# A combine in fp32r with a low part, single and half chunks of expert weights, and a norm vector spread by TensorE

## The reference, cut to what matters

```python
h = h + W_o( sum_i sigmoid(G_i xn) * P_i(mixer_i(xn)) )      # xn = RMSNorm(h)
h = h + hier_moe(rms_norm(h, norm2_g), ...)
return rms_norm(h, final_norm_g)

def hier_moe(x, wg, bg, we, be, w1, w3, w2):
    ...   # one of 4 groups, then the 2 best of its 8 experts: combine (256 x 32)
    for e in range(N_EXPERTS):
        h = jax.nn.silu(xt @ w1[e]) * (xt @ w3[e])
        out = out + combine[:, e:e + 1] * (h @ w2[e])
```

## Time and profile before

| | us |
|---|---|
| median of 3 runs | 423.47 (423.26 to 424.98) |
| the profiled execution | 424.43 |
| its span | 422.6 |
| TensorE busy | 392.2 (93%) |
| VectorE / ScalarE / GpSimd busy | 200.6 / 141.8 / 20.1 |
| bytes moved | 140.3 MB, 332 GB/s over the span |
| mean granted clock of TensorE | 0.985 |

### The profile page before, as it was taken

One profiled execution on the slowest core, in us unless ns is written; L12 is line 12 of the kernel. 1 busy time (PEld: TensorE's weight loads), 2 busy tenths in 40 slices (PEclk: granted clock), 3 DMA queues, 4 the chain that ended last, 5 costly groups with the idle time before them and its releaser, 6 DMA issues.

```text
span 422.6 us, 7127 instructions
## 1 busy us (share of the span) xinstructions
PE 392.2 (93%) x2826; PEld 263.9 (62%) x2826; DVE 200.6 (47%) x392; ACT 141.8 (34%) x257; POOL 20.1 (5%) x39
## 2 busy tenths in 40 slices
PE   6999999999999999999989999999999779679792
PEld 5998988677777777878765545453546335135251
DVE  3847574999888595673362323231222203112113
ACT  6734352638555535341430303030303012011014
POOL 3010000200000000000510000000000000000002
PEclk9999999999999999999999999999999989899898
DMA  8999999534352485569987999999999999999962
GB/s 295 421 406 352 399 382 395 198 136 158 106 186 99 152 347 200 205 243 365 420 359 268 433 425 426 410 424 426 426 428 428 426 426 430 426 428 426 430 267 99
DMA packets 16440, 140.29 MB, mean 332 GB/s; under 512 B 2081, under 2 KB 2465, under 8 KB 5025
## 3 DMA queue, kind: packets, MB, share of 16 engines
q1 hardware_dynamic: 15264, 138.07, 81.1%
q10 hardware_dynamic: 1152, 1.88, 1.2%
HBM read 138.90 MB, written 1.05 MB: 331 GB/s over the span
## 4 chain that ended last, share of the span: by engine, by line
PE 73%; DMA 18%; DVE 6%; issue 1%; POOL 0%; ACT 0%; POOLq 0%; DVEq 0%; SPq 0%
DMA ring<-in_experts 17%; PE bank L1758 10%; PE bank L1719 5%; PE bank L1785 5%; PE bank L1795 5%; PE bank L1525 5%; PE bank L1526 4%; PE bank L1527 4%; PE bank L1383 4%; PE bank L1384 4%; PE bank L1385 4%; PE bank L1646 2%; PE bank L1368 2%; PE bank L1647 2%; PE bank L1648 2%; PE bank L1487 1%
## 5 line engine op out<-in xcount | busy, mean ns | idle before, releaser
L1758 PE MATMUL bank<-ring,kv 128*32 128x512 f32 x512 | 65.9, 630 | 12.9 <-DMA ring<-in_experts 12.8
L458 DVE TENSOR_TENSOR part<-ring,part 128x2048 fp32r<-128x2048 f32 (+1 forms) x26 | 57.4, 2213 | 18.7 <-ACT part L451 18.6
L451 ACT CAST part<-ring 128x2048 fp32r<-128x2048 f32 (+1 forms) x26 | 48.0, 1847 | 32.5 <-DMA ring<-in_front 32.5
L1323 DVE TENSOR_TENSOR h<-h,bank 128x256 f32<-128x256 f32 x64 | 26.9, 421 | 60.6 <-PE bank L1795 60.3
L1719 PEld LDWEIGHTS bank<-qcur,att 128*128 128x128 f32 x256 | 31.6, 191 | 24.2 <-issue 24.2
L1758 PEld LDWEIGHTS bank<-ring,kv 128*32 128x32 f32 x512 | 13.7, 112 | 42.1 <-issue 29.7
L1525 PE MATMUL bank<-part,xhi 128*128 128x512 f32 x96 | 39.2, 408 | 0.0
L894 ACT ACTIVATE cw<-bank 128x256 f32<-128x256 f32 x8 | 3.1, 384 | 105.4 <-PE bank L1758 105.4
L1719 PE MATMUL bank<-qcur,att 128*128 128x128 f32 x256 | 38.4, 288 | 0.0
L1527 PE MATMUL bank<-part,xlo 128*128 128x512 f32 x96 | 37.5, 391 | 0.0
L1526 PE MATMUL bank<-part,xhi 128*128 128x512 f32 x96 | 37.5, 391 | 0.0
(11 more groups left out here) (250 smaller groups left out, 549.9 us busy)
## 6 DMA issues: line engine op xcount, KB each, us to landing
ring<-in_experts SPq DMA_DIRECT2D x35, 2048.0 KB, 27.6
ring<-in_front SPq DMA_DIRECT2D x28, 1024.0 KB, 5.6
ring<-in_experts SPq DMA_DIRECT2D x26, 1024.0 KB, 8.7
ring<-in_front SPq DMA_DIRECT2D x4, 512.0 KB, 6.9
ring<-in_projs SPq DMA_DIRECT2D x4, 512.0 KB, 5.0
ring<-in_front SPq DMA_DIRECT2D x2, 560.0 KB, 8.7
h<-in_x SPq DMA_DIRECT2D x2, 512.0 KB, 3.8
con<-in_vecs ACTq DMA_DIRECT2D x2, 512.0 KB, 7.5
```

The source lines that it names most:

```text
L451: nc.scalar.copy(high(n, half)[:, 0:c].bitcast(F32R), raw(n, half)[:, 0:c]).then_inc(hi_done, 1)
L458: nc.vector.tensor_tensor(low(n, half)[:, 0:c].bitcast(F32R), raw(n, half)[:, 0:c], high(n, half)[:, 0:c], ALU.subtract).then_inc(split_do ...
L1758: ins = mm(bank[0][CAP * e:CAP * (e + 1)], xgT[:, q, CAP * e:CAP * (e + 1)], expert(j, q, e), start=(q == 0), stop=(q == NQ1 - 1))
```

## The change

- **Combine.** The weighting leaves the scatter. VectorE makes `cmbT` a matrix of zeros and ones and sums `share`, the weight of each slot (a slot holds one token, so a row of it has at most one entry). ScalarE's copy scales by `share` and rounds to fp32r; a new VectorE operation, `low_part`, writes what the rounding left out, also fp32r. Each fp32 product becomes two fp32r ones. `combine` waits for `ylo_done`.
- **Pieces.** The output columns go in five pieces, 256, 256, 256, 128 and 128, in place of four of 256.
- **The transposes of `selw`** stand behind q2 instead of ahead of q0.
- **The last block of a round** has its gathers for the next block behind q4, q5, q6 and q7 (one k each) and no fillers; combine(1) stands ahead of second(2), combine(2) ahead of second(3).
- **SyncE** fetches the first six chunks after the prefetch one by one (`SINGLES`), and the last chunk of a round in two halves of 512 KB. The arrays in memory are laid out for that.
- **The last norm's vector** comes as a 128x256 tile (128 KB, four different rows repeated), early, into `wg`; four fp32 products with a spread column of the identity bring it to all partitions, ScalarE copies it out of PSUM. Five fillers remain of eight there.
- VectorE's sums and the squares behind the last block have one step more.

```diff
+PIECES = ((0, 256), (256, 512), (512, 768), (768, 896), (896, 1024))
+NP = len(PIECES)
...
+SINGLES = 6
...
+        ylo = (over("ylo0", [P, 512], "qT", 512), over("ylo1", [P, 512], "rw"))
...
+        cmbT = over("cmbT", [P, T], "vbd")[:]
+        share = stat[:, 40:41]
...
+        def columns(p):
+            return slice(*PIECES[p])
+        def low_out(p):
+            c0, c1 = PIECES[p]
+            return ylo[c0 // 512][:, c0 % 512:c0 % 512 + c1 - c0]
+        def second_out(p, rows):
+            return bank[4 + p % 2][rows, 0:PIECES[p][1] - PIECES[p][0]]
+        def combined(p, t):
+            return bank[6 + t][:, 0:PIECES[p][1] - PIECES[p][0]]
...
-            for c in range(SLOTS, NC - 2, 2):
+            for c in range(SLOTS, SLOTS + SINGLES):
+                sp.wait_ge(expert_used, earlier(c) + 1)
+                sp.dma_start(ring[:, AT[c]], single(c)).then_inc(expert_in[AT[c] // 2] if c % 2 else single_in, 16)
+            for c in range(SLOTS + SINGLES, NC - 2, 2):
                 sp.wait_ge(expert_used, earlier(c + 1) + 1)
                 sp.dma_start(slots_of(c), experts[c // NQ, c % NQ // 2]).then_inc(expert_in[AT[c] // 2], 16)
-            for c, sem_in in ((NC - 2, expert_in[AT[NC - 2] // 2]), (NC - 1, last_in)):
-                sp.wait_ge(expert_used, earlier(c) + 1)
-                sp.dma_start(ring[:, AT[c]], single(c)).then_inc(sem_in, 16)
+            ends = experts.rearrange("(r b) q p c -> r b q (p c)", b=ROUND)[:, ROUND - 1, NQ // 2 - 1]
+            one = ends[:, 0:P * ECHUNK].rearrange("r (p c) -> r p c", p=P)
+            halves = ends[:, P * ECHUNK:2 * P * ECHUNK].rearrange("r (i p c) -> r i p c", i=2, p=P)
+            def next_to_last(r):
+                sp.dma_start(ring[:, AT[NC - 2]], one[bass.ds(r, 1)].rearrange("o p c -> (o p) c")).then_inc(expert_in[AT[NC - 2] // 2], 16)
+            def last_chunk(r):
+                for i, sem_in in ((0, last_half_in), (1, last_in)):
+                    sp.dma_start(ring[:, AT[NC - 1], i * (SLOT // 2):(i + 1) * (SLOT // 2)],
+                                 halves[bass.ds(r, 1), i].rearrange("o p c -> (o p) c")).then_inc(sem_in, 16)
+            sp.wait_ge(expert_used, earlier(NC - 2) + 1)
+            next_to_last(0)
+            sp.wait_ge(expert_used, earlier(NC - 1) + 1)
+            last_chunk(0)
...
+                    act.wait_ge(mix_full, 1)
+                    act.dma_start(flat(wg[:]), lastrows).then_inc(last_rows_in, 16)
...
-            act.wait_ge(xn2_done, NT)
-            act.dma_start(fing, vecs[1:2].to_broadcast([P, D])).then_inc(vec_in, 16)
...
+            act.wait_ge(fing_full, 1)
+            for half in range(2):
+                nc.scalar.copy(fing[:, half * HALF:(half + 1) * HALF], bank[(7, 2)[half]][:]).then_inc(fing_done, 1)
...
+            def second_copy(after, p):
+                act.wait_ge(ye_full, after * NP + (p + 1))
+                act.wait_ge(cmb_done, after)
+                nc.scalar.activation(yN[:, columns(p)].bitcast(F32R), second_out(p, slice(0, P)), ACT.Copy, scale=share).then_inc(yn_done, 1)
...
             last_square(0, 1)
             second_copy(blocks, 3)
-            for n in (1, 2):
+            second_copy(blocks, 4)
+            for n in (1, 2, 3):
...
-                nc.vector.tensor_copy(cmbT, bank[1][:, 0:T]).then_inc(cmb_done, 1)
+                nc.vector.tensor_scalar(cmbT.bitcast(F32R), bank[1][:, 0:T], 0.0, None, ALU.is_gt)
+                nc.vector.tensor_reduce(share, bank[1][:, 0:T], AX.X, ALU.add).then_inc(cmb_done, 1)
...
+                def low_part(p):
+                    dve.wait_ge(yn_done, b * NP + (p + 1) + 1)
+                    nc.vector.scalar_tensor_tensor(low_out(p).bitcast(F32R), second_out(p, slice(0, P)), share, yN[:, columns(p)],
+                                                   ALU.mult, ALU.subtract).then_inc(ylo_done, 1)
+                def add(p):
                     for t in range(NT):
-                        dve.wait_ge(comb_done, b * (NT * NQT) + (NT * qt + t + 1))
-                        hv = h[:, t, qt * QC:(qt + 1) * QC]
-                        nc.vector.tensor_tensor(hv, hv, combined(t), ALU.add).then_inc(add_done, 1)
+                        dve.wait_ge(comb_done, b * (NT * NP) + (NT * p + t + 1))
+                        hv = h[:, t, columns(p)]
+                        nc.vector.tensor_tensor(hv, hv, combined(p, t), ALU.add).then_inc(add_done, 1)
+                low_part(0)
+                for p in range(1, NP):
+                    low_part(p)
+                    add(p - 1)
+                add(NP - 1)
...
-            keep_busy(8, ident, con[:, K_TRI:K_TRI + 2 * P])
+            pe.wait_ge(last_rows_in, 16)
+            for c in range(4):
+                row = ident[:, c:c + 1].to_broadcast([P, P])
+                ins = mm(bank[(7, 2)[c // 2]][:, (c % 2) * 256:(c % 2 + 1) * 256], row, flat(wg[:]), start=True, stop=True)
+            ins.then_inc(fing_full, 1)
+            keep_busy(5, ident, con[:, K_TRI:K_TRI + 2 * P], bank[6])
...
-                    pe.wait_ge(sel_done, b + 1)
-                    pe.wait_ge(hT_done, b + 1)
-                    for t in range(NT):
-                        ins = nc.tensor.transpose(bank[1][:, t * P:(t + 1) * P], flat(selw[:, t]), ident)
-                    ins.then_inc(cmb_full, 1)
...
-                        if j == ROUND - 1 and 4 <= q < NQ1 - 1:
-                            pe.wait_ge(add_done, b * (NT * NQT) + 5)
-                            keep_busy(2, ident, con[:, K_TRI:K_TRI + 2 * P])
-                    pe.wait_ge(sel_step, b + 2)
-                    gather(0, 1)
+                        if q == 2:
+                            pe.wait_ge(sel_done, b + 1)
+                            pe.wait_ge(hT_done, b + 1)
+                            for t in range(NT):
+                                ins = nc.tensor.transpose(bank[1][:, t * P:(t + 1) * P], flat(selw[:, t]), ident)
+                            ins.then_inc(cmb_full, 1)
+                        if j == ROUND - 1 and q >= 4:
+                            pe.wait_ge(sel_step, b + 2)
+                            gather(q - 4)
+                    if j < ROUND - 1:
+                        pe.wait_ge(sel_step, b + 2)
+                        gather(0, 1)
...
-                    gather(2)
+                    if j < ROUND - 1:
+                        gather(2)
                     pe.wait_ge(hT_done, b + 2)
-                    def second(qt):
-                        have_expert(j, NQ1 + qt)
+                    def second(p):
+                        if j == ROUND - 1 and p == NP - 2:
+                            pe.wait_ge(last_half_in, bb * 16 + 16)
+                        else:
+                            have_expert(j, NQ1 + PIECES[p][0] // QC)
                         for ht in range(HT):
                             for e in range(EB):
-                                ins = mm(second_out(qt, slice(CAP * e, CAP * (e + 1))), hT[:, ht, CAP * e:CAP * (e + 1)],
-                                         second_weights(j, qt, ht, e), start=(ht == 0), stop=(ht == HT - 1))
+                                ins = mm(second_out(p, slice(CAP * e, CAP * (e + 1))), hT[:, ht, CAP * e:CAP * (e + 1)],
+                                         second_weights(j, p, ht, e), start=(ht == 0), stop=(ht == HT - 1))
                         ins.then_inc(ye_full, 1)
-                    def combine(qt):
-                        pe.wait_ge(yn_done, b * NQT + (qt + 1) + 1)
-                        pe.sem_inc(expert_used, 1)
+                    def combine(p):
+                        pe.wait_ge(ylo_done, b * NP + (p + 1))
+                        if p != NP - 2:
+                            pe.sem_inc(expert_used, 1)
                         for t in range(NT):
-                            pe.wait_ge(add_done, b * (NT * NQT) + (NT * qt + t + 4))
-                            mm(combined(t), cmbT[:, t * P:(t + 1) * P], yN[:, qt * QC:(qt + 1) * QC],
-                               start=True, stop=True).then_inc(comb_done, 1)
+                            pe.wait_ge(add_done, b * (NT * NP) + (NT * p + t + 6))
+                            picked = cmbT[:, t * P:(t + 1) * P].bitcast(F32R)
+                            mm(combined(p, t), picked, yN[:, columns(p)].bitcast(F32R), start=True, stop=False)
+                            mm(combined(p, t), picked, low_out(p).bitcast(F32R), start=False, stop=True).then_inc(comb_done, 1)
                     second(0)
-                    gather(3)
-                    for qt in range(1, NQT):
-                        second(qt)
-                        combine(qt - 1)
-                    combine(NQT - 1)
+                    if j < ROUND - 1:
+                        gather(3)
+                    second(1)
+                    combine(0)
+                    if j == ROUND - 1:
+                        combine(1)
+                    second(2)
+                    combine(2 if j == ROUND - 1 else 1)
```

(9 more changed lines are left out.)

85 lines of the change are left out of this document (46 added, 39 removed).

## The result

| | before | after |
|---|---|---|
| median, 20 runs each, same chip | 424.35 us (423.26 to 426.21) | 425.05 us (424.71 to 426.7) |
| ratio to before, 95% interval | | 1.0018 (1.001 to 1.0026) |
| profiled execution | 424.43 us, span 422.6 | 424.9 us, span 422.7 |
| run's time less its span, median | 1.80 us | 2.16 us |

The kernel is 0.7 us (0.18%) slower: within half a per cent, and above the range that was given. Forecast was a gain of 2.0 us.

A forecast was written before the change was run, and what follows sets the result against it. The expert-weight stream plus a closing chain on TensorE, ScalarE and VectorE was taken as the bound. Second product 0 gains 4.2 us, the chain loses 2.2: 423.47 - 2.0 gives 421.5 us, range 420.0 to 423.5.

The forecast's parts named there:

- q0 and the first refill: First block: q0 starts at 219.8 instead of 220.91, the first refill is issued at 220.9 against 224.12.
- The vector's part: Before the stream's gap: dropping the 512 KB broadcast saves 1.2 us of stream, but the gap only opens sooner; worth nothing.
- I take the whole 3.2 us: Six single refills after the prefetch: the stream starts 3.2 us earlier (2.7 to 3.5) and all DMA bound landings move as much.
- S: Start of second product 0 in the last block: forecast at 401.95 against 406.12, 4.2 us earlier.
- It gains nothing: TensorE waits for the stream anyway: Combines in the blocks: the TensorE time saved by fp32r products brings no gain in the kernel's time.
- Some 2 us out of a block: TensorE, four combines of a block: fp32r products take 0.48 us per combine, where fp32 took about 1.1 per piece.
- The chain: Last block, from second product 0's start to the final scaling: 13.4 us against 11.2, a loss of 2.2 us.
- The prices of ScalarE and VectorE: Per-piece costs behind second product 0: scaled copy 0.49, low part 0.48, add 0.42 us; at 128 columns 0.40, 0.35, 0.29.
- An fp32r product of 128 columns: Combine products on TensorE in the last block: taken at 0.20 us, between 0.06 and 0.27.
- The clock: Rival, chance 0.07: with fillers gone TensorE falls to its low clock from second product 0 on; scaling 420.9, time 427.0 us.
- the stream does not keep the gain: Rival, chance 0.12: first three singles each lose about 1 us awaiting receipts, landings as before; scaling 418.55, time 424.7 us.
- the final scaling: ScalarE's scaling at the end of the last block: forecast to start at 415.35 against 417.31, 2.0 us earlier.

The follow-up runs named there:

- ring: The changed kernel with a new ring map: chunks 40 to 43 go to slots 18 to 21, 44 to 47 to slots 8 to 11; 423.35 us, 0.9982.
- the pairs of kernels above: With the new ring map: changed kernel against kernel before, landing 393.37 against 395.12 us; kernel before with six singles against without, 394.18 against 395.12.
- turn_first: The changed kernel with new ring map, regular last-block order, fp32 combine, and the transposes put back ahead of q0; 422.10 us, 0.9949 of the kernel before.
- order_ring: The changed kernel with the new ring map and the last block's combines ordered as in other blocks; 422.13 us, 0.9949 of the kernel before.
- the singles: The kernel before with only six single chunks after the prefetch in place of three pairs, old ring map; 424.82 us, 1.0012.
- the map: The kernel before with only the new ring map (chunks 40 to 43 to slots 18 to 21, 44 to 47 to 8 to 11); 423.64 us, 0.9986.
- fing_dma: The changed kernel with the last norm's vector fetched by the 512 KB transfer as before, eight fillers; 425.32 us, 1.0027 of the kernel before.
- best_fing_dma: The changed kernel with new ring map, regular last-block order, fp32 combine, and the last norm's vector by the 512 KB transfer; 421.48 us, 0.9929.

## Why the prediction failed

1. **q0 and the first refill: right.** 219.62 and 220.74, said 219.8 and 220.9. The vector's part was worth nothing, as said: in the router phase TensorE's fillers end at 216.06 and the rank product starts at 216.31 with 0.25 us to spare; ScalarE's copies begin at 216.00.
2. **"I take the whole 3.2 us. Later refills wait for slots that TensorE, ahead of the stream, has freed long before": wrong, and this is the step that failed.** The first refill was issued 3.4 us earlier, the landings of the last block came only 0.9 us earlier (395.38 to 394.50). Two losses make up the 2.5 us: the gate at chunk 40, 1.1 us at this landing (394.50 to 393.37, ring against after) and 1.3 at S; and the slow start of the stream, 1.2 to 1.5 us by the pairs of kernels above, whose cause stays open. The reuse of slots was to be read off the map line by line; I looked only at the first refills. The row was in the trace of before: two slices of 328 GB/s at 270 us and SyncE's issue at 268.47, too weak to matter there, and exactly what a stream 3 us earlier would run into. The rows I showed ended at 260 us.
3. **"It gains nothing: TensorE waits for the stream anyway"** was wrong for the same reason. Up to 270 us TensorE's pace sets when the gate opens. Nor did a block get 2 us shorter: it takes 20.9 us, before 20.7. "Some 2 us out of a block" failed twice. The four fp32r products of a combine take 0.67 to 0.76 us (411.15 to 411.91 in the last block), not 0.48. And the combines wait, 1.3 us in a block, mostly for adds. With the fp32 combine in the same program a block takes 21.4, so fp32r saves 0.6. With the transposes back ahead of q0 as well (turn_first) it is 21.2; what makes up the other 0.5 us over 20.7, the five pieces or something else, was not tried.
4. **S is set by its pair's landing: right**, but the landing was 404.4, not 401.95.
5. **The chain: nearly right.** 13.0 us, said 13.4, before 11.2. The prices of ScalarE and VectorE held: copy 474 and 368 ns (said 0.49 and 0.40), low part 484 and 350 (0.48 and 0.35), add 414 and 285 (0.42 and 0.29). An fp32r product of 128 columns starts 0.11 to 0.17 us after its neighbour, where I took 0.20, but one of 256 up to 0.22 (the 0.76 us above), where I took 0.12. So the near hit of the sum owes something to errors of opposite sign.
6. **The clock stayed up in the last block.** The windows of the kernel after (us, busy us of PE, PEld, DVE, ACT and POOL, granted clock, DMA share, GB/s) show the full 2.4 GHz with TensorE busy 0.85 of 2 us. In the block before, from 366 to 374 us, it was at 0.50 to 0.72:

```profile
410.00:412.00 2.00, 0.85 (x8) 0.69 (x12) 1.14 (x3) 1.12 (x4) 0.50 (x1) 1.00 0.00 0
412.00:414.00 2.00, 1.24 (x34) 0.97 (x34) 0.98 (x4) 1.47 (x5) 0.78 (x1) 1.00 0.00 0
```

7. **The rival "the stream does not keep the gain"** (0.12) came nearest with its 424.7, and partly by luck: it had the final scaling at 418.55, 1.1 us later than it was, and the 0.36 us outside the span and the low first median made up for that. It had only a part of the mechanism: the gate, the other half of the loss, it did not name. A loss at the start of the single chunks it did name, and there is one of 1.2 to 1.5 us, but no run here shows that a receipt is its cause. The Trainium skill (DMA: Bandwidth & Descriptors, Anatomy of one DMA) gives each transfer a fixed cost of about 2.0 us beside its bytes; its figure is for transfers that GpSimd issues, and these are SyncE's. By it three pairs made six singles would have lost 6 us; the runs do not agree with that per transfer, since all six together lose at most 1.5.

In numbers: S came 2.5 us later than forecast, the chain was 0.4 shorter, so the final scaling came 2.1 late; the 0.36 us outside the span, which no row inside it could show, bring this to 2.4 of the 2.7 us between the forecast gain of 2.0 and the measured loss of 0.7. The remaining 0.3 is inside what the runs leave open. One slip of the prediction bears on nothing: what isn't TensorE's in the chain of the earlier trace rows is 27%, not 23. Against the median of before on the longer series, 424.35 in place of 423.47, the forecast would have been 422.4: 0.9 us of the distance in absolute time is the short first series.

The Trainium skill (ScalarE: Activation LUTs, What ACT_TABLE_LOAD costs) says that each operand of one value per partition adds some 93 ns to an ACTIVATE. The traces nearly agree: the scaled copy of the changed kernel against the plain one of fp32 takes 474 against 372 ns at 256 columns and 368 against 266 at 128, both 102 more, though the scaled one also rounds to fp32r, which no run has apart. Three such copies stand on the chain behind S in the changed kernel and in order_ring.

## What to carry to other kernels

Before moving the start of a stream through a ring of buffers, write down for each refill which chunk it replaces and when that one is read: a stream can be no earlier than its worst slot, and a gate that costs nothing now is the next bound once the stream starts earlier. An edit that seems worthless (the singles, 1.0012, or the map, 0.9986) can be one half of a pair, so try the pair. And where one step feeds two clocks, as the fp32r combine (shorter on TensorE, longer through ScalarE and VectorE), it should be priced again once the bound has moved: it went from neutral to a likely loss.

## What the runs showed that was not expected

- A stream restarted from empty with single transfers of 1 MB is slow to fill: 33, 90, 164, 377 GB/s in its first slices, and a dip to 295 and 262 after 7 us, where pairs of 2 MB later hold 427. By the bytes moved up to 235 us, 1.0 to 1.3 of the 1.2 to 1.5 us of landing that it loses are lost by then. Pairs of 2 MB have such a low slice too, 229 GB/s two us after their issue. The cause was not settled.
- The changed kernel and all its variants spend 0.36 us more outside the span than the kernel before and its variants, the same in every run to about 0.1 us but for fing_dma; the cause is open, and so is that of its 2.42 us, since best_fing_dma with the same exchange has 2.18.
- The granted clock stayed at 1.00 through the last block with no filler left in it, where the kernel before fell to 0.55 at 396 us with its fillers.
